# Hybrid decoder step: u and v rows of an expert in one 8 KB gather, one ring, sums by diagonal matrices

## What is computed

```python
experts = e1 * PEER_KEYS + e2
g = jax.nn.softmax(vs, axis=-1)
act = jax.nn.gelu(jnp.einsum('nd,nhkd->nhk', xb, peer_u[experts]), approximate=False)
return jnp.einsum('nhk,nhkd->nd', g * act, peer_v[experts])
```

## Time and profile before

| | |
|---|---|
| Median of 3 runs | 3542.61 us (3528.41 to 3545.09) |
| Span of the profiled execution | 3534.4 us |
| Bytes moved by DMA | 1321.73 MB, 1107.43 MB of them by POOL's gathers |
| Busy | PE 2634.4, DVE 2374.2, POOL 2393.4, ACT 433.3 us |

### The profile page before, as it was taken

The page is one execution under the profiler, slowest core; times in us unless marked ns, Lnnn a source line. Parts: engine busy times, 40 slices in busy tenths (PEclk is TensorE's granted clock), DMA queues, the critical chain, the costliest instruction groups (busy, mean ns, idle before and its releaser), DMA issues.

```text
span 3534.4 us, 35434 instructions
## 1 busy us (share of the span) xinstructions
PE 2634.4 (75%) x11810; PEld 1284.3 (36%) x11810; DVE 2374.2 (67%) x6243; ACT 433.3 (12%) x980; POOL 2393.4 (68%) x2118
## 2 busy tenths in 40 slices
PE   6658676788867798797766777797877778767656
PEld 5634123553432344362232223463332234313211
DVE  4686667667678786767478765867478766847642
ACT  1101100113101231111001110111001110000000
POOL 0155776667757776657767777657767776677876
PEclk8879779898888989899889888999888999988799
DMA  6478999999999999999999999999999999999999
GB/s 252 169 277 313 367 349 408 352 397 369 366 404 362 380 348 408 407 400 377 380 411 402 388 377 409 395 412 395 381 410 397 396 399 407 397 408 384 322 410 371
DMA packets 372025, 1321.73 MB, mean 374 GB/s; under 512 B 60674, under 2 KB 72130, under 8 KB 351618
## 3 DMA queue, kind: packets, MB, share of 16 engines
q0 software_dynamic: 304128, 1107.43, 81.0%
q1 hardware_dynamic: 67714, 212.03, 15.4%
HBM read 1311.41 MB, written 7.88 MB: 373 GB/s over the span
## 4 chain that ended last, share of the span: by engine, by line
POOL 26%; PE 25%; DMA 22%; DVE 15%; issue 10%; SPq 2%; ACT 1%; DVEq 0%; POOLq 0%; ACTq 0%
POOL v_ring L818 13%; POOL u_ring L805 12%; DMA v_ring<-down_rows,codesT 12%; PE ps L863 8%; PE ps L927 6%; DMA u_ring<-up_rows,codes 6%; DMA wbuf<-weights 4%; DVE u_ring L1775 3%; DVE arena L1745 3%; PE ps L917 2%; PE ps L1127 2%; PE ps L1180 2%; DVE idx L1745 1%; DVE top_c L1745 1%; DVE top_v L1745 1%
## 5 line engine op out<-in xcount | busy, mean ns | idle before, releaser
L863 PE MATMUL ps<-v_ring,Z 128*32 128x512 f32 x4096 | 1324.0, 688 | 606.6 <-DMA v_ring<-down_rows,codesT 479.3
L1775 DVE CUSTOM_DVE_ANT_0 u_ring<-u_ring,xn 128x1024 f32<-128x1024 f32 x1056 | 1260.7, 1219 | 596.0 <-DMA u_ring<-up_rows,codes 595.5
L805 POOL DMA_INDIRECT u_ring<-up_rows,codes x1056 | 1191.4, 1128 | 676.6 <-issue 305.8
L818 POOL DMA_INDIRECT v_ring<-down_rows,codesT x1056 | 1200.8, 1137 | 449.3 <-issue 297.9
L863 PEld LDWEIGHTS ps<-v_ring,Z 128*32 128x32 f32 x4096 | 242.9, 118 | 1404.0 <-DMA v_ring<-down_rows,codesT 836.4
L927 PE MATMUL ps<-wbuf,xT 128*128 128x256 f32 (+2 forms) x1184 | 287.4, 401 | 64.8 <-DMA wbuf<-weights 36.5
L1127 PEld LDWEIGHTS ps<-xT,wbuf 128*128 128x128 f32 x2176 | 269.0, 202 | 160.8 <-issue 106.8
L1127 PE MATMUL ps<-xT,wbuf 128*128 128x128 f32 (+1 forms) x2176 | 292.1, 290 | 38.9 <-DMA wbuf<-weights 38.8
L927 PEld LDWEIGHTS ps<-wbuf,xT 128*128 128x128 f32 (+1 forms) x1184 | 226.8, 198 | 139.8 <-DMA wbuf<-weights 41.1
L1745 DVE MAX8 vals<-arena 128x8 f32<-128x128 f32 (+1 forms) x288 | 69.0, 280 | 113.9 <-ACT arena L1560 113.3
L917 PE MATMUL ps<-wbuf,kT 128*128 128x256 f32 (+1 forms) x480 | 104.7, 371 | 0.0
(11 more groups left out here) (332 smaller groups left out, 2358.2 us busy)
## 6 DMA issues: line engine op xcount, KB each, us to landing
wbuf<-weights SPq DMA_DIRECT2D x142, 1024.0 KB, 8.3
u_ring<-up_rows,codes POOLq DMA_INDIRECT x1056, 8.6
v_ring<-down_rows,codesT POOLq DMA_INDIRECT x1056, 8.8
u_ring<-weights SPq DMA_DIRECT2D x8, 1024.0 KB, 14.7
v_ring<-weights SPq DMA_DIRECT2D x8, 1024.0 KB, 14.9
wbuf<-weights SPq DMA_DIRECT2D x9, 768.0 KB, 7.5
resid<-x_prompt SPq DMA_DIRECT2D x8, 512.0 KB, 7.0
table<-decay_in SPq DMA_DIRECT2D x8, 512.0 KB, 10.3
```

Of the source, the lines that this page charges most:

```text
L805: pool.indirect_dma_start(out=u_ring[:, i % U_RING, :], out_offset=None, in_=up_rows, in_offset=bass.IndirectOffsetOnAxis(ap=codes[:, t % ...
L818: pool.indirect_dma_start(out=v_ring[:, v % V_RING, :], out_offset=None, in_=down_rows, in_offset=bass.IndirectOffsetOnAxis(ap=codesT[:, t ...
L863: mm = pe.matmul(acc[32 * c:32 * c + 32, half, :], (Zs if t == TILES else Z)[:, at:at + GS], v_ring[:, v % V_RING, half * 512:(half + 1) * ...
L1775: dve.tensor_tensor_reduce(u, u, xn[:, t % 2], 1.0, 0.0, ALU.mult, ALU.add, dots[:, k:k + 1]).then_inc(dot_done, 1)
```

## The change

1. u and v rows stand side by side in one table of 16384 rows of 8 KB (`expert_rows`, laid out ahead of the launch). A slot is one gather of 128 rows of 8 KB into one ring of nine places of 8 KB a partition (`RING`). The dot reads the first half of a place, PE the second half. A gather waits for the sums nine slots before.
2. Slots keep the position on the partition, for v too. POOL forms for every slot a 128x128 diagonal matrix, identity times gelu times gate (`make_diag`), into five places (`DIAGS`). PE adds a slot with two matmuls of 128 columns.
3. The gelu is taken in place in pieces of up to 4 slots, up to 2 slots behind the bound of the site (`GELU_LAG`); PE adds up to 3 slots behind it (`SUM_LAG`).
4. Gates are computed head by head: DVE negates the largest value, ACT takes the exponential with its sum, DVE takes the reciprocal and multiplies.
5. `Z`, the coefficients, the transposed numbers, and their instructions are gone. The lists of sizes stay, but for `LAST`.

The core of the diff:

```diff
-GROUPS, GS = 4, 32
-U_RING, V_RING = 8, 9
+GS = 32
+RING, DIAGS = 9, 5
+GELU_LAG, SUM_LAG = 2, 3
...
-        LAST = [9, 9, 5, 3, 3, 3] + [3, 3] * H + [2, 2] + [58]
+        LAST = [5, 5, 5, 4, 4, 4] + [3, 4] * H + [3, 3] + [21 + SUM_LAG]
...
+            def gather(i):
+
+                t, k = divmod(i, SLOTS)
+                if i < 8:
+                    pool.wait_ge(piece_done, PIECE_AT[0, O_0 + i] + 1)
...
+                if i >= RING:
+                    pool.wait_ge(v_done, i - RING + 1)
                 pool.indirect_dma_start(
+                    out=ring[:, i % RING, :], out_offset=None, in_=expert_rows,
                     in_offset=bass.IndirectOffsetOnAxis(ap=codes[:, t % 2, k:k + 1], axis=0),
+                ).then_inc(row_in[i % RING], 16)
+
+            def make_diag(i):
...
+                pool.wait_ge(gelu_done, i + 1)
+                if i >= DIAGS:
+                    pool.wait_ge(v_done, i - DIAGS + 1)
+                of, m = (stack, ST) if t == TILES else (ident, P)
+                pool.tensor_scalar(diag[:, i % DIAGS, 0:m], of[:], dots[:, k:k + 1], gates[:, t % 2, k:k + 1],
+                                   ALU.mult, ALU.mult).then_inc(diag_ready, 1)
+
+            rows = TILES * SLOTS + GS
+            for i in range(RING):
+                gather(i)
...
+            for i in range(DIAGS - 1):
+                make_diag(i)
+            for i in range(RING, rows):
+                make_diag(i - RING + DIAGS - 1)
+                gather(i)
...
+            def add_row(i):
...
+                pe.wait_ge(diag_ready, i + 1)
+                for c in range(2):
+                    mm = pe.matmul(acc[0:n, c, :], diag[:, i % DIAGS, 0:n], ring[:, i % RING, D + c * 512:D + (c + 1) * 512],
+                                   start=False, stop=(k == slots_of(t) - 1))
+                mm.then_inc(v_done, 1)
...
+            def rows_added(done, upto):
+                for i in range(max(done - SUM_LAG, 0), max(upto - SUM_LAG, 0)):
+                    add_row(i)
...
+            def gelu(first, end):
+
+                t = first // SLOTS
+                at = slice(first - t * SLOTS, end - t * SLOTS)
+                act.wait_ge(dot_done, end)
+                act.activation(dots[:, at], dots[:, at], ACT.Gelu).then_inc(gelu_done, end - first)
...
+            def gelus_and_sums(done, upto):
+
+                at, end = max(done - GELU_LAG, 0), min(max(upto - GELU_LAG, 0), SLOTS * TILES)
+                while at < end:
+                    to = min(end, at + 4, (at // SLOTS + 1) * SLOTS)
+                    gelu(at, to)
+                    at = to
...
-                dve.wait_ge(u_in[i % U_RING], 16 * (i // U_RING + 1))
-                u = u_ring[:, i % U_RING, :]
+                dve.wait_ge(row_in[i % RING], 16 * (i // RING + 1))
+                u = ring[:, i % RING, 0:D]
...
+                do_signal(gate_in, H * t + h + 1, dve.tensor_scalar, gate_n[0:n, h:h + 1], top_v[0:n, h, 0:1], -1.0, None, ALU.mult)
+
+            def take_gates(t, h, n):
+                dve.wait_ge(gate_exp, H * t + h + 1)
...
+                do(dve.reciprocal, gate_s[0:n, h:h + 1], gate_s[0:n, h:h + 1])
+                do_signal(gates_ready, H * t + h + 1, dve.tensor_scalar, gates[0:n, t % 2, h * K:(h + 1) * K], gate_x[0:n, h],
+                          gate_s[0:n, h:h + 1], None, ALU.mult)
```

More of the change, by code:

```diff
@@ L1594, in projected @@
                 slots()
-                gate_exps(t - 1, P)
+                for h in range(HEADS_HERE, H):
+                    gate_exps(t - 1, h, P)
                 for _ in range(3):
@@ L1727, in _ @@
             act.wait_ge(first_in, 32)
-            slots = Pace(groups)
+            slots = Pace(gelus_and_sums)
             for t in range(TILES):
@@ L1732, in _ @@
             sample_rest(slots)
-            gelu(TILES, 0)
-            make_Z(TILES, 0)
+            for k in range(0, GS, 4):
+                gelu(TILES * SLOTS + k, TILES * SLOTS + k + 4)
             put_y(TILES)
```

264 lines of the change are left out of this document (84 added, 180 removed).

## The result

| | before | changed |
|---|---|---|
| median of the runs | 3539.61 us (3528.41 to 3545.09, 4 runs) | 4357.57 us (4353.67 to 4369.95, 4 runs) |
| ratio, 95% interval | | 1.2346 [1.23, 1.2391] |
| span of the profiled execution | 3534.4 us | 4368.2 us |

The changed kernel is slower by 818 us. The forecast was 3800 us with a range of 3430 to 4150: the direction was right, the size a third of what came. TensorE's granted clock does not explain the loss: it is 0.891 on the mean in the changed kernel's profile and 0.87 to 0.89 in the runs of before on the three chips where it takes 3534 to 3540 us.

The account below looks back on a forecast made before the run. The prediction took DMA to bound the kernel, kept there by the depth of gathers ahead. Its terms summed as 3534 + 229 - 38 + 10 + 110 - 50 = 3795, plus 8 for the runs' median: about 3800 us, range 3430 to 4150.

Parts of the forecast that it names:

- Part 2: GpSimd's order, gathers behind diagonals: VectorE's idle time for rows becomes 824 us in place of 595.5, +229.
- The stall of 6.25 us at the fourth place: In sites of 4 or 5, VectorE idles for a row whose gather was not issued: 91 x 6.25 = 569 us.
- Sites of three: Third gather leaves late and its row is wanted in the next site: stall 2.0 us, times 59 sites, 118.
- The end: After the last dot only a gelu, a diagonal and two matmuls follow, some 3 us: -38.
- Sites of 1 and 2 wait for nothing new: Sites with one or two slots were taken to add no new waits for rows.
- Part 5: TensorE's sums cost 1.0 us a slot as before: 0; earlier keys for VectorE's top-k: -50; ScalarE's added table loads: 0 beyond Part 2.
- Rival 4: TensorE becomes the bound, if narrow matmuls in column groups ran side by side, a factor of four: 5500 us; chance 0.02.
- Part 4: VectorE: small operations +10; dots held by GpSimd's diagonals, half of a 232 us bound, +110.
- Part 1: Gathers in rows of 8 KB reach 429 GB/s in place of 411: 116 us where DMA stays full, lower bound 0.
- The table loads: ScalarE's gelu table load behind the wait for dots, 0.55 us for each of 41 pieces of four: 23 us.
- Rivals 1 and 2: First: DMA stays the bound, faster, 3426 us, chance 0.20. Second: landing plus diagonal take 3.7 us, around 3540, chance 0.12.
- Rival 3: GpSimd and VectorE block each other: diagonals take 0.94 us, each dot is held by 0.22: 4165 us; chance 0.12.

Follow-up runs that it names:

- e2: Changed kernel with gelu pieces cut where the previous site's dots end, gathers still behind diagonal i - 5: 4025.9 us, ratio 1.1358.
- e6: Kernel before the change with only 4 of its 8 u places and 5 of its 9 v places used: 3771.5 us, ratio 1.0667.
- e11: Changed kernel with sums up to 5 slots behind in place of 3, nothing else: 4173.8 us, 1.1357 where before takes 3667.
- e1: Changed kernel with gather i issued behind diagonal i - 8 in place of i - 5: 4278.1 us, ratio 1.2093.
- e8: Changed kernel with gelu pieces cut and gathers behind diagonal i - 7, sums still three slots behind: 3982.4 us, ratio 1.1272.
- r2: Changed kernel with gelu pieces cut, gathers behind diagonal i - 7 and sums five slots behind: 3647.8 us, ratio 1.0328.
- e15: Changed kernel with gelu pieces cut and ScalarE forming the diagonals in place of GpSimd, lag of sums three: 3721.0 us, 1.0017 where before takes 3712.8.
- e16: Changed kernel with gelu pieces cut, ScalarE forming the diagonals and sums four slots behind: 3599.4 us, 0.9685 where before takes 3712.8.
- e4: Changed kernel without the second half of each sum but for a tile's last slot: 4269.0 us.
- e5: Changed kernel with gathers behind diagonal i - 8, gelu pieces cut, and second half of sums left out but for a tile's last slot: 3889.5 us.
- e9: Changed kernel with Copy in place of Gelu, cutting ScalarE's table loads from 242 to 1: 4271.4 us, ratio 1.2068.

## Why the prediction was right and wrong

**Right: the ring of waits, and, with some luck, its price.** Part 2 put 7.4 us from the end of dot N + 1 to the landing of row N + 3. The timeline above has 7.06 (2601.43, where the accumulator is read, to 2608.49). The gather left after 1.16 us, not 1.8, and landed 0.3 later than the 5.6 put. But this turn is quicker than most. Over the 80 sites of four the way from the end of dot N + 1 to the start of dot N + 3 is 8.4 us on the mean, 2.2 to the gather's start and 6.2 from there, 1.0 more than put. The stall came out right all the same, since dot N + 2, which the sum let run at once, waited 1.10 us itself. The stall of 6.25 us at the fourth place measured 6.04 in 80 sites and 5.96 in 12: 555 us for the 569 of the sum (91 sites were reckoned, 92 are there). Sites of three took 131 us (118), the last site and the sample 118 (98; the last site has 21 dots, not the 24 reckoned). The end became 33 us shorter (38): the last dot ends 14 us before the span's end, against 47. The nine places were hardly ever the limit, 44.2 us. A diagonal took 0.45 us at its median (0.35). The tiles `ring` and `diag` of the changed kernel (durations ns min/median/max):

```profile
L790 POOL DMA_INDIRECT ring<-expert_rows,codes x1056: 937/1014/2425, 138.5 to 4345.2; - x176
L1735 DVE CUSTOM_DVE_ANT_0 ring<-ring,xn x1056: 1194/1224/1568, 160.7 to 4352.8; 128x1024 f32<-128x1024 f32 x176
...
  PE ps L843: 44.2, 79
...
DMA to landing us min/median/max: 5.4/8.0/17.4
```

```profile
L806 POOL TENSOR_SCALAR diag<-ident,dots,gates x1024: 438/452/3359, 164.8 to 4246.8; 128x128 f32<-128x128 f32 x171
```

**The step that failed: "Sites of 1 and 2 wait for nothing new", and rows already issued at zero.** Part 2 set its 824 us of new waits in place of the 595.5 of before, as if those went. They stayed and grew. Places ahead of the fourth take 259 us in sites of two (174 before), 9 in sites of one, and 207 + 22 in the first three places of sites of four and five: 497 of the 510 us by which 1334 exceeds 824. In before the same places took 324 us: these the sum dropped, and 173 are new. The sum let rows N to N + 2 be there when the site began. The timeline shows how they are not: a gather that leaves late lands late, and the ones behind it at DMA's pace, their dots 2.5 to 3.1 us apart (2608.49, 2611.04, 2614.13, 2616.61), so the next site finds its rows just landing. I priced the stall as if it came out of a full queue. That the refill behind a stall is the whole of it is not shown, and e2 speaks against it: it took 262 us from the fourth places and only 13 from those ahead of them. e6 has 488 us in these places with no order of diagonals at all, half the depth and 129 us in its fourth places. So it is rather that few rows are ahead, at every site, which the sum priced only where a row was not issued at all.

**What I had not in the sum: the lag.** Part 2 placed gather behind diagonal behind dot, but did not follow the same chain to TensorE: with sums three slots behind, PE stands in the site for it (846.4 and 1159.8 us). In the table it shows only as +78 us of VectorE's waits for TensorE, and yet e11 took 184 to 200 us off the changed kernel by a longer lag alone. So the sum had at nothing a cost that, by that run, is about a quarter of the 818. How it splits from the waits for rows is open, as the two hide each other: with the order mended and the lag left, the waits for TensorE are 815 us (e1). Two slots more of lag measure 335 us from e8 to r2, one slot more 122 from e15 to e16.

**Part 5, TensorE at 0: two misreadings.** The stream of sixteen records in 4.02 us is four slots of two matmuls each: in these traces a float32 matmul stands as two records. The text ahead of the prediction says four matmuls to a slot; `v_round` issues two, one for each half, and 1056 slots have 4224 records before and after alike. So the 0.5 us of the 64 wide ones is half a matmul, and two matmuls a slot cost not 1.0 but twice that.

The second misreading is the clock. The stream of 4.02 us stands behind 3.96 us of idle time of PE and ran at a granted clock of 0.50, the lower level of 1.2 GHz; streams of the same kind at 1.00 take 1.94 us. Before, PE in order of time and the windows of two such streams (columns as in the earlier trace rows):

```profile
694.22 1.94 PE L863 MATMUL ps<-v_ring,Z 128*32 128x512 f32 x16
```

```profile
694.20:696.10 1.90, 1.90 (x18) 0.48 (x17) 1.90 (x6) 1.76 (x2) 0.18 (x1) 1.00 1.00 401
2447.30:2451.30 4.00, 3.98 (x17) 1.18 (x17) 2.37 (x4) 0.00 (x0) 3.10 (x3) 0.50 1.04 411
```

In the changed kernel, one slot in order of time, the window around it, and the whole group:

```profile
2610.23 1.88 PE L843 MATMUL ps<-ring,diag 128*128 128x512 f32 x4
```

```profile
2609.00:2612.00 3.00, 3.00 (x14) 1.52 (x12) 2.29 (x4) 0.60 (x1) 0.00 (x0) 1.00 1.02 421
```

```profile
L843 PE MATMUL ps<-ring,diag 128*128 128x512 f32 (+1 forms) x4224 | 2254.7, 679 | 849.8 <-POOL diag L806 846.4
```

At the same clock sixteen narrow records take 1.94 us and four wide ones 1.88. One record lasts 0.59 us at its median, so the four start (1.88 - 0.59) / 3 = 0.43 apart, 1.7 us a slot; the narrow ones start four together, every 0.43 us, which is 0.43 a slot. So in such a stream the narrow matmuls of before did overlap fourfold. The Trainium skill (TensorE: Matmul & The Clock Gate, Part 3 on row and column tiling), which the prediction set aside as contradicted, is borne out by that stream.

The group's busy time grew by less than fourfold, from 1324.0 + 36.2 to 2254.7 us: +894. In before full fours are not the rule: 1591 of the 4096 records start within 0.05 us of the one ahead, where in full fours three of four would. And 800 of the 4224 records last over 0.8 us, at the lower clock; in the changed kernel 694 do. In the turn above PE stood idle 4.37 us for a diagonal, and then its weight loads and matmuls went 0.85 us apart in place of 0.43, at a granted clock of 0.55:

```profile
2602.41 7.12 PE L843 MATMUL ps<-ring,diag 128*128 128x512 f32 x12 [4.37 <-POOL diag L806]
...
2603.14 0.34 PEld L843 LDWEIGHTS ps<-ring,diag 128*128 128x128 f32 x1 [0.43 <-issue]
...
2603.99 0.34 PEld L843 LDWEIGHTS ps<-ring,diag 128*128 128x128 f32 x1 [0.52 <-issue]
```

```profile
2602.40:2605.70 3.30, 3.29 (x5) 1.31 (x6) 1.23 (x2) 0.00 (x0) 2.86 (x4) 0.55 0.44 92
```

Rival 4 had the factor of four right, and its chance of 0.02 rested on the two misreadings. Its price was wrong: four times the 1.0 us of the low clock, 4.0 a slot, where 1.7 to 2.1 (2254.7 / 1056) came. So TensorE did not become the bound, and PE's gaps took most of the growth: what leaving out half of it gives back is 89 us by e4 and 196 by e5, both at a lower clock. The keys came earlier by 21 us (113.3 to 91.8), not 50.

**Part 4, the dots: +110 not there.** The median dot is 1.224 us, 1.222 before, the group's busy time is 1278.4 us against 1260.7: +18. It is the diagonal that is held, up to 3.36 us, its mean half above its median (683.6 us of busy time over 1024: 0.67). The 330 diagonals that overlap a dot take 0.96 us at their median, the 491 that overlap nothing of VectorE 0.45; the dots that overlap a diagonal take 1.24 on the mean, the others 1.22, the longest 1.57. The Trainium skill (SBUF — State Buffer, "Who interferes with whom") says that the two kinds contend, and the trace agrees; the time was lost almost wholly on GpSimd's side, where the prediction reckoned it on VectorE's. The small operations came to +33 in place of +10.

**Part 1.** DMA was not kept full, so no gain, as the sum had it. Where it was full again, in e16, single slices of the page move 420 GB/s, those of before at most 411: 2%, for the 4% that the earlier trace rows suggested.

**The table loads** are worth 86 us by e9, of which the sum had 23. So Part 5's "0 beyond the term in part 2" was some 60 short.

**The rivals.** Rivals 1 and 2 needed a DMA share near 1 or a landing with its diagonal in 3.7 us; a middle stretch of the changed kernel (columns as in the earlier trace rows) has a share of 0.81, where I had put 0.9:

```profile
2000.00:2500.00 500.00, 371.17 (x1177) 190.39 (x1177) 277.32 (x708) 80.10 (x163) 231.99 (x261) 0.88 0.81 309
```

Rival 3 gave the nearest time, 4165, and half its mechanism is there: diagonals beside a dot take 0.96 us, where it put 0.94. But its mark, all diagonals near 1 us or dots above 1.4, was not met; of the 80 diagonals on which a fourth row hung only 17 took over 0.7 us, and its 122 us for held dots did not come. Rival 4 is told above.

In one line: forecast +261 in the span, measured +834; of the 573 missing, 509 are waits for rows, nearly all at places where the sum let the row be there, 128 are the waits for TensorE and ScalarE (+78, where -50 was put), and the dots give 92 back. The rest, 28, is VectorE's other work (+23) and the end (+5).

## What to carry to other kernels

When two streams of work share an in-order queue, follow each item's chain once around: if a transfer stands behind work that needs an earlier transfer, the depth is what this distance allows, not the number of buffers; and moving the dependent work to an engine that has no transfers behind it (e15: some 261 us) did more here than any order tried at the same lag. When the depth shrinks, price it at every place and not only where a row is missing altogether: waits seen before do not vanish into the new one (324 us became 497). Follow the chain to every engine that waits on it: a lag that was left short cost as much as a quarter of the loss. And before taking a duration of a matmul from a row, count its records per source line and look at the granted clock of that stretch: one stream of sixteen took 4.02 us at 0.50 and another 1.94 at 1.00.

## What the runs showed of the hardware

- A gather of 128 rows of 8 KB costs GpSimd about as much to issue as one of 4 KB: 937/1014 ns (min/median) against 933/938, with means of 1117 and 1128.
- Before takes 3535, 3667 and 3713 us on different chips, while one kernel with 8 KB rows took 3651.8 and 3647.8 us on the second and the first. What makes before slow there is not settled, as there is no trace of it on those chips; that it is the 4 KB packets is only a guess. Its mean granted clock is lower there too, 0.84 to 0.86 against 0.87 to 0.89, whether as cause or as effect.
- ScalarE forms a diagonal of 128 x 128 in 0.397 us (mean, e16; the gate is multiplied in by an instruction of its own) and GpSimd in 0.668, with 0.45 at its median. Beside a dot of VectorE GpSimd's takes 0.96 at its median and ScalarE's 0.39.
- Sixteen float32 records of 32 columns by 512, in four column groups, take 1.94 us at a granted clock of 1.00, four records of 128 columns 1.88 us.
- Behind 4.37 us of idle time TensorE's granted clock was 0.55 for the next 3.3 us, and its float32 records of 512 columns went 0.85 us apart in place of 0.43.
- A table load of ScalarE takes 1.283 us in all 242 cases; in the changed kernel it starts 18 ns behind the instruction before it and the next starts 12 ns behind it, both at the median.
